# A two-layer hybrid encoder on one core: attention of the last layer asks only for the 512 kept positions

## The reference, cut to what matters

```python
h = concatenate([meta, x], axis=1)                 # 16 learned tokens + 512 positions = 528
for l in range(DEPTH):                             # 2 layers
    hn = rms_norm(h, attn_norm_g[l]); proj = hn @ w_in[l]      # columns for four mixers
    y_a = mla_mixer(...)     # latent attention, 8 heads: q, k of width 96, v of 64
    y_b = ssd_mixer(...)     # two-way state space
    y_c = diff_mixer(...)    # differential attention, 4 heads of two maps each, v of 128
    y_d = mlstm_mixer(...)
    h = h + concatenate([y_a, y_b, y_c, y_d], -1) @ w_out[l]
    hn = rms_norm(h, ffn_norm_g[l])
    gate, up = split(hn @ w_ffn_in[l], 2, axis=-1)
    h = h + (silu(gate) * up) @ w_ffn_out[l]
return h[:, N_META:]                               # N_META = 16: these rows are dropped
```

## Time and profile before

| | us |
|---|---|
| median of 3 runs | 2311.18 (2311.1 to 2311.18) |
| profiled execution, its own time | 2310.49 |
| its span | 2308.7 |
| TensorE busy | 2110.4 (91%) |
| VectorE busy | 1083.4 (47%) |
| GpSimd busy | 997.0 (43%) |
| ScalarE busy | 845.4 (37%) |
| mean granted clock of TensorE | 0.974 |

### The profile page before, as it was taken

How to read it: one execution, slowest core, us unless ns; L and a number is a source line. 1 busy time by engine, 2 the same in 40 slices (tenths; PEclk the granted TensorE clock), 3 DMA queues, 4 the chain that set the end, 5 groups by cost and what they waited for, 6 DMA issues and landing times.

```text
span 2308.7 us, 33441 instructions
## 1 busy us (share of the span) xinstructions
PE 2110.4 (91%) x13634; PEld 1819.6 (79%) x13634; DVE 1083.4 (47%) x1699; ACT 845.4 (37%) x1400; POOL 997.0 (43%) x592
## 2 busy tenths in 40 slices
PE   7999998888778999999989999988887789999999
PEld 7888886566667999999988888875665567888887
DVE  8632355565565644441056322545655656444400
ACT  3322343566553322222223222435665543222221
POOL 4365333674312344444434554336743124444444
PEclk9999999999999999999999999999999899999999
DMA  4211111000001233223322211120000013233233
GB/s 158 65 56 56 56 46 64 10 1 19 28 19 37 92 92 91 88 89 100 100 75 64 65 56 56 38 73 10 1 19 19 19 46 92 91 94 98 91 109 110
DMA packets 40039, 143.85 MB, mean 62 GB/s; under 512 B 4432, under 2 KB 4560, under 8 KB 39760
## 3 DMA queue, kind: packets, MB, share of 16 engines
q1 hardware_dynamic: 39888, 141.72, 19.6%
HBM read 139.60 MB, written 2.10 MB: 61 GB/s over the span
## 4 chain that ended last, share of the span: by engine, by line
PE 73%; DVE 13%; ACT 8%; issue 4%; POOL 1%; DMA 1%; ACTq 0%; SPq 0%; DVEq 0%; POOLq 0%
PE pb L800 46%; PE pb L831 6%; PE pb L830 6%; PE pb L832 6%; ACT ebuf L1384 2%; DVE kh L1781 2%; PE pb L1226 2%; DVE proj L1763 1%; ACT ebuf L1395 1%; ACT rstd L1359 1%; PE pb L1082 1%; ACT rstd L1360 1%; DVE mbuf L1849 1%; PE pb L930 1%; DVE proj_r L1857 1%
## 5 line engine op out<-in xcount | busy, mean ns | idle before, releaser
L584 POOL TENSOR_TENSOR parts<-raw,parts 128x1024 fp32r<-128x1024 f32 x248 | 604.9, 2440 | 835.1 <-ACT parts L1435 834.8
L800 PE MATMUL pb<-mix,parts 128*128 128x264 f32 x4608 | 670.4, 294 | 41.0 <-POOL parts L584 17.6
L800 PEld LDWEIGHTS pb<-mix,parts 128*128 128x128 f32 x4608 | 608.9, 193 | 66.6 <-issue 28.8
L1435 ACT ACTIVATE parts<-raw 128x1024 fp32r<-128x1024 f32 x248 | 262.5, 1058 | 824.1 <-PE pb L800 522.4
L800 PE MATMUL pb<-proj_r,parts 128*128 128x264 f32 x3104 | 428.0, 286 | 0.5 <-POOL parts L584 0.5
L800 PEld LDWEIGHTS pb<-proj_r,parts 128*128 128x128 f32 x3104 | 400.0, 189 | 0.8 <-issue 0.7
L830 PE MATMUL pb<-proj_r,parts 128*128 128x512 f32 x528 | 207.6, 393 | 0.8 <-DVE mbuf L1763 0.8
L832 PE MATMUL pb<-proj_r,parts 128*128 128x512 f32 x528 | 207.8, 394 | 0.0
L831 PE MATMUL pb<-proj_r,parts 128*128 128x512 f32 x496 | 198.1, 399 | 0.0
L1769 DVE TENSOR_TENSOR h<-h,pb 128x528 f32<-128x528 f32 (+1 forms) x48 | 33.3, 694 | 270.7 <-PE pb L800 138.2
L1763 DVE TENSOR_TENSOR mbuf<-pb,rstd 128x528 f32<-128x528 f32 (+1 forms) x44 | 30.8, 699 | 214.1 <-PE pb L800 109.8
(11 more groups left out here) (273 smaller groups left out, 2932.5 us busy)
## 6 DMA issues: line engine op xcount, KB each, us to landing
raw<-w_stream SPq DMA_DIRECT2D x250, 512.0 KB, 3.5
w_head<-w_heads SPq DMA_DIRECT2D x8, 512.0 KB, 4.9
h<-x_t SPq DMA_DIRECT2D x8, 264.0 KB, 6.5
out_t<-h SPq DMA_DIRECT2D x8, 256.0 KB, 4.8
con<-consts SPq DMA_DIRECT2D x1, 1652.5 KB, 10.3
par<-params SPq DMA_DIRECT2D x1, 340.0 KB, 4.2
con<-consts SPq DMA_DIRECT2D x1, 128.0 KB, 6.8
```

The costliest lines, as they stand in the source:

```text
L584: nc.gpsimd.tensor_tensor(parts[:, n % PARTS, 1, :], w, parts[:, n % PARTS, 0, :].bitcast(FP32), ALU.subtract).then_inc(split.sem, 1)
L800: last = nc.tensor.matmul(pb[rows_, 2 * p + a, 0:HALF], lhs_t, rhs[:, a * HALF:(a + 1) * HALF], start=start, stop=stop)
L1435: nc.scalar.activation(parts[:, n % PARTS, 0, :], raw[:, r % RAW, :], ACT.Copy).then_inc(lead_ready.sem, 1)
```

## The change

In the last layer the queries become four tiles of 128, positions 16 to 143, 144 to 271 and so on (`q_tiles`). So there are 32 latent and 16 differential units instead of 40 and 20; keys stay at 528. The first layer keeps its five tiles. attend becomes one product of 512 columns in bank 6 in place of two of 264 (`attended`), and evacuations, squares, norms and splits of these outputs cover 512 columns. What the fifth step carried is respread: `prepare` starts with stage 3 at tile 0; the dense pieces of heads 6 and 7 are (0,3), (3,6), (6,8) in tiles 1 to 3; those of the first differential pair (0,2), (2,4), (4,6), (6,8), those of the other pairs (0,2), (2,5), (5,8) in tiles 1 to 3. Residual adds move from i = 4 to i = 3.

```diff
+        def q_tiles(layer):
+            return TILES if layer < DEPTH - 1 else [(N_META + i * P, P) for i in range(SEQ // P)]
+        def n_q(layer):
+            return len(q_tiles(layer))
+        def queried(layer, ap):
+            return ap[:, N_META:T] if layer == DEPTH - 1 else halves(ap)
+        def query_sums(layer, rows_=slice(0, P)):
+            return pb[rows_, 6, 0:SEQ] if layer == DEPTH - 1 else pair(3, rows_)
...
-        def dense_part(u):
-            hp, i = u // NT, u % NT
+        def dense_part(layer, u):
+            hp, i = u // n_q(layer), u % n_q(layer)
+            if layer == DEPTH - 1:
+                return ((0, 2), (2, 4), (4, 6), (6, 8))[i] if hp == 0 else (None, (0, 2), (2, 5), (5, 8))[i]
             if hp == 0:
                 return ((0, 2), (2, 4), (4, 6), (6, 7), (7, 8))[i]
             return (None, None, (0, 3), (3, 6), (6, 8))[i]
+        def out_part(layer, i):
+            if layer == DEPTH - 1:
+                return (None, (0, 3), (3, 6), (6, 8))[i]
+            return (None, (0, 2), (2, 4), (4, 6), (6, 8))[i]
...
-        def prepare(prep, n):
-            hd, i = n // NT, n % NT
+        def prepare(prep, layer, n):
+            hd, i = n // n_q(layer), n % n_q(layer)
             if hd + 2 < MLA_H:
-                for stage in ((), (3,), (4,), (0, 1), (2,))[i]:
+                stages = ((), (3,), (4,), (0, 1), (2,)) if layer < DEPTH - 1 else ((3,), (4,), (0, 1), (2,))
+                for stage in stages[i]:
                     prep(stage, hd + 2)
...
+                cut = slice(N_META if k >= KD and l == DEPTH - 1 else 0, T)
+                lead, other = (ap[:, cut] for ap in mixed_parts(k))
...
+                def attended(lhs_t, rhs, start, stop):
+                    if l < DEPTH - 1:
+                        return product(3, lhs_t, rhs, start, stop)
+                    return nc.tensor.matmul(query_sums(l), lhs_t, rhs[:, N_META:T], start=start, stop=stop)
...
-                for n in range(N_ATT_M):
-                    hd, i = n // NT, n % NT
-                    if n + 2 < N_ATT_M:
+                for n in range(n_att_m(l)):
+                    hd, i = n // n_q(l), n % n_q(l)
+                    if n + 2 < n_att_m(l):
                         scores(n + 2)
...
-                    if hd + 2 >= MLA_H and i:
+                    if hd + 2 >= MLA_H and out_part(l, i):
...
-                        beside(l, G_OUT1 + g, 0, mixed_parts, ((2 * i - 2, 2 * i),))
+                        beside(l, G_OUT1 + g, 0, mixed_parts, (out_part(l, i),))
...
-                    if dense_part(u):
+                    if dense_part(l, u):
                         pe.wait_ge(rs_ready.sem, rs_ready.at(l, RS_OD + hp))
-                        beside(l, G_OUT1 + 3 + hp, 0, mixed_parts, (dense_part(u),))
+                        beside(l, G_OUT1 + 3 + hp, 0, mixed_parts, (dense_part(l, u),))
...
-                    if i == NT - 1:
+                    if i == n_q(l) - 1:
                         residual(l, G_OUT1 + 3 + hp, 3 + hp)
```

More of the change, by code:

```diff
@@ L341, in turned_sums, with turned_tail @@
             return pb[:, TURN, 0:NT * TILES[-1][1]].rearrange("p (j q) -> p j q", q=TILES[-1][1])
-        def turned_tail(tile0):
-            return proj_r[0:TILES[-1][1], (tile0 + NT - 1) * T:(tile0 + NT - 1) * T + 512]
+        def turned_tail(layer, tile0):
+            a = (tile0 + NT - 1) * T + q_tiles(layer)[0][0]
+            return proj_r[0:TILES[-1][1], a:a + 512]
         def tail_sums():
@@ L1236, in attend @@
                             both = v_parts[:, j, m * P:(m + 1) * P]
-                            product(3, both, lead, j == 0, False)
-                            last = product(3, both, rest, False, j == NT - 1)
+                            attended(both, lead, j == 0, False)
+                            last = attended(both, rest, False, j == NT - 1)
                         else:
                             c = (m - MLA_H) * 2 * P
-                            product(3, v_parts[:, j, c:c + P], lead, j == 0, False)
-                            product(3, v_parts[:, j, c:c + P], rest, False, False)
-                            last = product(3, v_parts[:, j, c + P:c + 2 * P], lead, False, j == NT - 1)
+                            attended(v_parts[:, j, c:c + P], lead, j == 0, False)
+                            attended(v_parts[:, j, c:c + P], rest, False, False)
+                            last = attended(v_parts[:, j, c + P:c + 2 * P], lead, False, j == NT - 1)
                     last.then_inc(o_ps.sem, 1)
@@ L1285, in _ @@
                 pe.wait_ge(tr_evac.sem, tr_evac.at(l, TR_DV + NT))
-                for u in range(DIFF_U):
-                    hp, i = u // NT, u % NT
-                    if u + 1 < DIFF_U:
+                for u in range(diff_units(l)):
+                    hp, i = u // n_q(l), u % n_q(l)
+                    if u + 1 < diff_units(l):
                         score_pair(u + 1)
@@ L1649, in _ @@
                 scaled_map(l, 0)
-                for n in range(N_ATT_M):
-                    hd, i = n // NT, n % NT
-                    if n + 1 < N_ATT_M:
+                for n in range(n_att_m(l)):
+                    hd, i = n // n_q(l), n % n_q(l)
+                    if n + 1 < n_att_m(l):
                         softmax(l, n + 1)
@@ L1754, in mixed_split @@
             def mixed_split(l, k):
-                lead, rest = mixed_parts(k)
-                link(nc.vector.tensor_copy(lead, tile_of(proj, MIXED[k])))
-                nc.vector.tensor_tensor(rest, tile_of(proj, MIXED[k]), lead.bitcast(FP32), ALU.subtract).then_inc(mixed.sem, 1)
+                cut = slice(N_META if l == DEPTH - 1 else 0, T)
+                lead, rest = (ap[:, cut] for ap in mixed_parts(k))
+                src = tile_of(proj, MIXED[k])[:, cut]
+                link(nc.vector.tensor_copy(lead, src))
+                nc.vector.tensor_tensor(rest, src, lead.bitcast(FP32), ALU.subtract).then_inc(mixed.sem, 1)
             def scale_out(l, g, dst):
@@ L1791, in normed, with normed_out @@
                 ins = nc.vector.scalar_tensor_tensor(out=src, in0=src, scalar=gain, in1=rstd2[rows_, :], op0=ALU.mult, op1=ALU.mult)
+                return ins.then_inc(rs_used.sem, 1) if count else ins
+            def normed_out(l, src, gain, count=True):
+                at = queried(l, src)
+                ins = nc.vector.scalar_tensor_tensor(out=at, in0=at, scalar=gain, in1=queried(l, rstd2[:, :]), op0=ALU.mult, op1=ALU.mult)
                 return ins.then_inc(rs_used.sem, 1) if count else ins
```

165 lines of the change are left out of this document (88 added, 77 removed).

## The result

| | us |
|---|---|
| before, median of 4 runs beside it | 2311.18 (2311.1 to 2315.46) |
| changed, median of 4 runs | 2299.94 (2296.96 to 2301.86) |
| ratio | 0.9949, 95% interval 0.9937 to 0.9961 |
| profiled execution of the changed kernel | 2299.14, its span 2297.3 |

A forecast was written before the change was run, and what follows sets the result against it. Latent heads were taken as bound by a chain through other engines, with TensorE nearly the bound; 10.2 + 5.1 + 0.5 - 1.05 + 2.9 + 0.3 = 17.95 us gained, giving 2293.2 us, 8 in 10 range 2284 to 2299.

The forecast's parts named there:

- heads 6 and 7: Last two latent heads, without preparation, TensorE last: 33.65 us together instead of 36.80, 3.1 us gained.
- the first differential pair: Head pair 0 keeps four rounds and loses the fifth; the next attend starts 5.1 us earlier.
- both stops: TensorE's waits in each latent head: about 1.0 us ahead of the key product, about 1.5 us ahead of attend.
- Rival 2: Latent heads and differential tiles: only removed work counts, new waits are filled; 34.8 us gained, 2276 us; chance 0.04.
- Rivals 3 and 4: Low clock in some latent heads (2298.6 us; 0.10 with GpSimd's rival), or as a rule, slower than before (2316.6; 0.03).
- Rival 5: Latent heads: GpSimd becomes the bound, 2294 to 2297 us; counted with the rival of some low-clock heads, together 0.10.
- Head 0: First latent head, no attend: key product 2.96 us earlier, 0.63 back, 2.3 us gained.
- pair 3: Last differential pair, no tile following: 25.75 us with the clock's cost instead of 28.62, 2.9 us gained.
- The wait of the dense products for the root: Pairs 1 to 3: dense pieces at the second tile wait 3.6 us for ACT's reciprocal root; low clock behind costs 1.8.
- the order norm, split, difference is moved as a whole, so I keep it: End of pairs 1 and 2: the difference meets a GpSimd split as before, taking 2.01 us.
- its last 0.3: Closing term of the sum: last attend and narrower splits, 0.3 us gained.
- the falls of the later attends: Attends behind stops of 2.8 us run at the low clock level: 1.55 us more in pairs 2 and 3.

The follow-up runs named there:

- e4: Changed kernel with the scores of the fourth tile in latent heads 0 to 5 moved one step earlier, between turn and key product; 2297.60 us.
- e7: Changed kernel with ScalarE making the query's root ahead of the scaling in the fourth step of latent heads 0 to 5; 2294.72 us.
- e1: Changed kernel with GpSimd's splits of the last layer's differential outputs 528 columns wide again; 2294.83 us.
- e9: Changed kernel with dummy products filling TensorE's stops ahead of the attends that open pairs 1 to 3; 2294.94 us.
- e10: Changed kernel with dummy products in both waits of the later pairs, ahead of the norm sum and ahead of the attends; 2288.26 us.
- e8: Changed kernel with later dense pieces, GpSimd's weight split ahead of its norm wait, and the query's root ahead of the scaling; 2273.14 us, ratio to before 0.9829.
- e0: The changed kernel run again without any edit; 2297.38 us.
- e2: Changed kernel with the dense pieces of pairs 1 to 3 behind the third and fourth turn, four and four, none at the second tile; 2281.22 us.
- e3: Changed kernel with 18 dummy products ahead of the norm sum in each later pair, where TensorE otherwise waits; 2293.22 us.

## Why the prediction was right and wrong

**Right: what bounds what.** The latent heads were costed as a chain and not as TensorE's work. The removed tile was put at 1.7 us of TensorE and 0.91 of time; 0.87 came (4.36 us in five periods), with both stops in their places and within 0.1 us of their sizes. e4 and e7 show the reason rather than the sum alone. Rival 2 (only removed work counts) would have needed 18.4 us a period. Rivals 3 and 4 expected a low clock there; the five periods ran at a granted clock of 1.00. Rival 5 (GpSimd) would have lengthened the period; it did not. Head 0, heads 6 and 7, the first differential pair, pair 3 and the end each hold within 0.25 us. The wait of the dense products for the root was 3.58 us for 3.6, and the collision aside the stop ahead of attend too: 2.71 in e1, where the difference is caught as before, for 2.8.

**Wrong: "the order norm, split, difference is moved as a whole, so I keep it".** The order held, the widths did not: the change itself takes 16 columns off GpSimd's two splits in front, and 0.08 us were enough for the weight split to catch the one-column product ahead of the scaling. This costs 0.95 us in each of pairs 1 and 2 (the stops of e1). The forecast took the narrower splits for a small gain (within its last 0.3) and did not follow what they move. The earlier trace rows has the split and the difference, but not the small product between them, which stood 0.06 us from being caught. A collision that depends on who starts first can't be carried over as a constant; its two outcomes, 1.24 and 2.18 us, should both have stood in the forecast.

**Wrong: the clock of the attend that opens pair 1.** It stands behind a stop of 1.40 us, and the earlier trace rows has an attend of 5.46 us behind just such a stop. I charged the falls of the later attends and not this one; it took 5.23 us, and in e9, with the stop filled, 3.74. That is 1.5 us. The other falls were right in kind: 1.57 for 1.8 behind the dense stop, 1.57 for 1.55 at the attends. 1.9 for the collision and 1.5 for this attend are the 3.4 us of pairs 1 and 2. e10 bears the sum out. Without any fall the forecast's pair is 26.0 us: 11.5 to the dense product, 7.3 to the fourth turn, 7.17 to the next attend. e10 has 11.60, 7.46 and 8.13, the last with the 0.95 of the collision in it. So the walk was 0.26 too short and the fall behind the dense stop 0.23 too long; that these two cancel in the sum is luck. Two figures of the forecast differ from its rows: a full tile's lead is given 0.60 us, where the earlier trace rows has 0.58, and pair 2 comes to -1.07, not -1.05. Neither moves the sum by more than 0.02.

**Wrong: the width of the range.** The three runs that were shown of before lay within 0.08 us, and I took that for what an execution varies by. The span up to T0 varies by 5.3 us in unedited code, and beside the experiments the kernel before took between 2309.3 and 2315.1 us. Of the first four executions of the changed kernel the profiled one was late at T0 (for the others this is not known); four more gave 2297.38, inside the range. With the 14.2 us that the change gives from T0, the profiled run of before leads to 2296.3. The miss of 6.7 us in the first median is thus 3.7 of the sum and, as an estimate, some 3 of the executions. Much of the variation ahead of T0 goes with TensorE's clock: worked out to four digits from the clock records of the traces, the granted clock up to T0 is 0.9761 in the earliest (e7) and 0.9707 in the latest (e8), and over the twelve profiles its correlation with T0 is -0.78. It is not the whole: e0 and e10 both have 0.9750, with T0 at 1582.31 and 1584.29. What makes the clock fall at other places from one execution to the next stays open.

**Missed: that the table of dense pieces was the costly part.** The forecast priced the wait for the root about right (2.9 + 1.8 us a pair, 14.1 in all; 14.8 came back in e2) and then let it stand as a cost of the change. e2 shows that the same change with the pieces one tile later is 16 us better. This cost is as large as the whole gain of the change from T0, 14.2 us.

## What to carry to other kernels

When a step is taken out of a pipelined loop, price the chain and the stops apart from the work, and put whatever the step carried behind the point where its bank or operand is free: a piece one place too early holds everything queued behind it, here 5 us a pair. A stop on TensorE can cost more than its length: in these pairs the lower clock behind six stops cost another 9.2 us, and dummy products in the stops brought them back. It need not: the stops of 0.91 and 1.40 us in the latent heads brought no low clock (1.00 over 95.95 us), so look at the granted clock behind a stop before filling it. Compare executions from the last common row ahead of the change, since what lies before it varies by more than the change's smaller terms.

## What the runs showed of the hardware

- **A one-column VectorE operation can take 2.34 us.** With two SBUF operands (`rsum` and `neg_lam`) it is held for the whole of a GpSimd operation of 128 x 1024 that began 0.02 us earlier. The reciprocal just ahead of it, with one operand, took its 0.14 us while GpSimd was busy with another split (1837.91). The Trainium skill (SBUF — State Buffer, SBUF: two separate sides) says that VectorE operations with two SBUF inputs and GpSimd operations that read SBUF share a port pair as an exclusive lock, held for the whole instruction by whichever starts first. The trace agrees, by the product that ended at 1841.51 with the split's end at 1841.49, and by e1, where the product that started 0.05 us ahead of the split took 0.16.
- **The same stop can be followed by either clock level.** Behind a stop of 1.40 us the attend of pair 1 took 5.23 us in the changed kernel and 3.73 in e4, whose program is the same from head 6 on. It took 5.07 to 5.30 us in eight of the nine profiles in which this stop is not filled. The Trainium skill (TensorE: Matmul & The Clock Gate, The HAM clock gate) says that the watch on the array's activity runs free of the program; such a pair of rows is what that would look like, and no run here shows the watch itself.
- **Filling a stop raises the clock.** In e10, 122 dummy products in six stops turned a granted clock of 0.88 into 1.00 and gave 9.2 us, although no wait ended earlier for them. Filling some of the stops did less than its share: 3.9 us in e3 for three falls of 1.57, and 3.1 in e9 for 4.7 expected, since a fall behind a stop that was left grew longer (an attend of 6.21 us for 5.31, a first dense product of 0.79 for 0.51).
